# Five dot products moved ahead of the second half's turned rows, and the second unit's expert choice begun four items later

## The reference, cut to what matters

```
def peer_layer(h, w_q, keys, u, v):
    q = (h @ w_q).reshape(B, S, PEER_HEADS, 2, PEER_KEY_DIM)
    sc = jnp.einsum('bshpd,phnd->bshpn', q, keys)
    v1, i1 = lax.top_k(sc[..., 0, :], PEER_TOPK)          # 16 of 128
    v2, i2 = lax.top_k(sc[..., 1, :], PEER_TOPK)
    cand = v1[..., :, None] + v2[..., None, :]            # 256 sums
    cidx = i1[..., :, None] * PEER_N_KEYS + i2[..., None, :]
    best, pos = lax.top_k(cand, PEER_TOPK)
    gates = softmax(best)
    ...
        ue = jnp.take(u, it, axis=0)
        act = gelu(einsum('tkd,td->tk', ue, ht))
        ve = jnp.take(v, it, axis=0)
        return einsum('tk,tkd->td', gt * act, ve)
```

## Time and profile before

| what | us |
|---|---|
| three timed runs, median | 1663.82 |
| lowest and highest | 1662.99, 1665.97 |
| the profiled execution, span | 1766.8 |
| PE busy in it | 1526.0 (86%) |
| DVE busy | 1053.5 (60%) |
| ACT busy | 647.2 (37%) |
| POOL busy | 551.6 (31%) |
| mean granted clock of PE | 0.927 |

### The profile page before, as it was taken

How to read it: one execution, slowest core, us unless ns; L and a number is a source line. 1 busy time by engine, 2 the same in 40 slices (tenths; PEclk the granted TensorE clock), 3 DMA queues, 4 the chain that set the end, 5 groups by cost and what they waited for, 6 DMA issues and landing times.

```text
span 1766.8 us, 20473 instructions
## 1 busy us (share of the span) xinstructions
PE 1526.0 (86%) x8043; PEld 1152.1 (65%) x8043; DVE 1053.5 (60%) x1889; ACT 647.2 (37%) x1016; POOL 551.6 (31%) x607
## 2 busy tenths in 40 slices
PE   8999999998999999999999898796676775777684
PEld 7999897887797999988898765452222332333231
DVE  5655655786655655567456676375555564656563
ACT  5444535794453544446444232221111121111111
POOL 1000001210000100000100457666666657666663
PEclk9999999999999999999999688898788889888787
DMA  8555554343353555654345779989999989999995
GB/s 278 189 185 181 160 174 159 97 144 119 129 170 111 186 182 189 188 182 149 115 144 167 275 261 364 354 327 366 362 369 371 367 317 392 378 363 365 362 363 224
DMA packets 199945, 431.95 MB, mean 244 GB/s; under 512 B 20773, under 2 KB 114090, under 8 KB 199850
## 3 DMA queue, kind: packets, MB, share of 16 engines
q0 software_dynamic: 73728, 268.47, 39.4%
q1 hardware_dynamic: 123456, 159.92, 27.9%
q10 hardware_dynamic: 2666, 2.26, 0.4%
HBM read 429.55 MB, written 1.05 MB: 244 GB/s over the span
## 4 chain that ended last, share of the span: by engine, by line
PE 60%; DVE 17%; issue 10%; another core or an unknown queue 6%; ACT 6%; DMA 1%; POOL 0%; ACTq 0%; DVEq 0%
PE ps L403 60%; DVE GS L2449 3%; DVE WL L1712 3%; ACT WH L1210 2%; DVE RAW L2449 2%; DVE AR L2449 1%; DMA GS<-in_peer_u_dram,AR 1%; DVE AR L2300 1%; DVE AR L2296 1%; DVE H L1754 1%; DVE XN L1749 1%; DVE AR L2302 0%; DVE AR L2298 0%; DVE XL L1768 0%
## 5 line engine op out<-in xcount | busy, mean ns | idle before, releaser
L1712 DVE TENSOR_TENSOR WL<-RAW,WH 128x2048 fp32r<-128x2048 f32 x143 | 328.0, 2294 | 259.0 <-ACT WH L1210 257.0
L403 PE MATMUL ps<-XH,WH 128*128 128x256 f32 (+1 forms) x1448 | 424.9, 293 | 17.0 <-issue 7.3
L403 PE MATMUL ps<-XH,WL 128*128 128x256 f32 (+1 forms) x1448 | 417.5, 288 | 5.4 <-issue 5.4
L403 PE MATMUL ps<-XL,WH 128*128 128x256 f32 (+1 forms) x1448 | 417.4, 288 | 5.0 <-issue 5.0
L403 PE MATMUL ps<-GS,AR 128*128 128x512 f32 x576 | 298.2, 666 | 123.6 <-issue 88.3
L1210 ACT ACTIVATE WH<-RAW 128x2048 fp32r<-128x2048 f32 x137 | 262.4, 1915 | 183.0 <-PE ps L403 181.2
L403 PEld LDWEIGHTS ps<-GS,AR 128*128 128x128 f32 x576 | 120.1, 214 | 289.7 <-issue 247.2
L403 PEld LDWEIGHTS ps<-XH,WH 128*128 128x128 f32 x1448 | 285.5, 197 | 25.5 <-issue 16.9
L403 PEld LDWEIGHTS ps<-XH,WL 128*128 128x128 f32 x1448 | 285.9, 197 | 8.0 <-issue 8.0
L403 PEld LDWEIGHTS ps<-XL,WH 128*128 128x128 f32 x1448 | 285.8, 197 | 7.6 <-issue 6.8
L2501 POOL TENSOR_TENSOR small<-small 128x1 f32<-128x1 f32 x28 | 15.4, 557 | 708.2 <-DVE small L1744 365.7
(11 more groups left out here) (372 smaller groups left out, 1887.1 us busy)
## 6 DMA issues: line engine op xcount, KB each, us to landing
RAW<-in_ffn_w_gu_dram SPq DMA_DIRECT2D x44, 1024.0 KB, 5.2
RAW<-in_w_in_dram SPq DMA_DIRECT2D x39, 1024.0 KB, 5.2
RAW<-in_ffn_w_down_dram SPq DMA_DIRECT2D x22, 1024.0 KB, 4.8
RAW<-in_w_out_dram SPq DMA_DIRECT2D x12, 1024.0 KB, 4.8
RAW<-in_xa_wkv_dram SPq DMA_DIRECT2D x8, 1024.0 KB, 5.3
RAW<-in_w_peer_q_dram SPq DMA_DIRECT2D x8, 1024.0 KB, 5.4
RAW<-in_xa_wq_dram SPq DMA_DIRECT2D x4, 1024.0 KB, 7.1
RAW<-in_xa_wo_dram SPq DMA_DIRECT2D x4, 1024.0 KB, 5.0
```

The costliest lines, as they stand in the source:

```text
L403: return nc.tensor.matmul(out_, lhsT, rhs, start=start, stop=stop, skip_group_check=True)
L1712: nc.vector.tensor_tensor(conv(1, k, kt), v, conv(0, k, kt).bitcast(F32), ALU.subtract).then_inc(S["lo"], 1)
```

## The change

The dot products of items 0 to 4 are called in DVE's `query`, behind `choose_first` and ahead of `turn_half(1)`; the loop over items skips them. The generator of unit 1's choice is still made at item 0, but its steps begin at item 5: the condition for a step is now `j >= AHEAD and kk > 0`. On ACT the gates of unit 1 are made at item 9 and no longer at item 5; all later units keep rank 5. Nothing is added to or removed from what is computed.

```
+    AHEAD = 5
...
-            if kk == 5 and n + 1 < 16:
+            if kk == (5 if n else 9) and n + 1 < 16:
                 gates(n + 1)
...
-            if kk > 0:
+            if j >= AHEAD and kk > 0:
                 next(nxt[0], None)
...
+                for j in range(AHEAD):
+                    item(j)
                 turn_half(1)
...
             if what == "items":
                 for j in n:
-                    item(j)
+                    if j >= AHEAD:
+                        item(j)
```

## The result

| | median us | runs | lowest to highest |
|---|---|---|---|
| kernel before | 1664.46 | 4 | 1662.99 to 1665.97 |
| changed kernel | 1683.00 | 4 | 1682.54 to 1683.62 |

The ratio is 1.0105, with a 95% interval of 1.0088 to 1.0122: 18.5 us slower, where 8 were forecast. The time lies in the range, close to that of the rival in which PE's clock falls (1684.8).

A forecast was written before the change was run, and what follows sets the result against it. The prediction took the nearly unbroken stream of 512 gathers at 411 GB/s as the bound. PE later 4.0 plus indices 4.8, less some 0.8 covered, gave +8 us: 1671.8, range 1660.5 to 1686.

The forecast's parts named there:

- the rival in which PE's clock falls: PE's pause before the second-half query, about 987.3 to 992.4, halves its clock: 13 on top of 8, 1684.8; chance 0.22.
- The reading of the bound: From 977 us on, 512 gathers at 411 GB/s, nearly unbroken in timed runs; breaks at the stream's start count in full.
- The 103 us: Profiled 1766.8 us against timed median 1663.82; fifteen units at 5.1 us, 77 us, were taken as waits absent from timed runs.
- PE later by 4.0 us: Five dot products ahead of the second turn delay PE's second-half query from about 988.4 to 992.4; 0 to 4.0, taken 4.0.
- Early gathers, 0: POOL's gathers waiting for the early dot products' buffers go out sooner; gain 0 to 4.5 us, taken as 0.
- Indices, 4.8 us: Second unit's choice four items later delays row 16's gather, indices at 1037.7; price 3.2 to 4.8 us, taken 4.8.
- Gates, 0: Gates at item 9 cost ScalarE two table loads of 1.28 us; free, at most 2.6 us, or 5.3 by the skill page.
- The sum, +8: Whole kernel: 4.0 plus 4.8, less some 0.8 covered by queued transfers, gives +8 us, 1671.8; chance 0.36.
- first term: PE's second-half query starting 4.0 us later, on the premise that timed runs lack the profile's wait giving cover.

The follow-up runs named there:

- choice_late: Kernel before with only the second unit's choice begun at item 5 and its gates made at item 9, dot products unmoved; 1667.28 us, ratio 1.0023.
- filler8: Changed kernel plus eight idle products (matmuls nobody reads) on PE ahead of the second half's query; 1672.30 us, ratio 1.0044.
- filler8_dots_only: Changed kernel with the choice caught up by item 8, gates at item 6, and eight idle PE products ahead of the second-half query; 1670.48 us, ratio 1.0023.
- before_warm_2: Kernel before with one idle product in each of three short PE pauses, repeated at the usual condition; 1662.31 us, ratio 0.9986.

## Why the prediction was right or wrong

- **The reading of the bound** was right: the stream of gathers at 411 GB/s sets the end, and what breaks it between 1002 and 1040 is lost. The 103 us by which the earlier trace rows exceeds the timed runs were indeed not in them; unit periods of 45.94 us are 40.7 there.
- **PE later by 4.0 us**: mechanism right, size 5.5 (988.02 to 993.51). 0.4 of the difference is that PE started at 988.02 before, not at 988.4. The rest is that the first dot product waited 1.06 us for its gather and started at 986.69, not 986.04, and that the five took 6.08 us and not 5.7.
- **Early gathers, 0**: right. V2 to V4 went out without a wait, and the next wait grew to 8.75 us.
- **Indices, 4.8 us**: mechanism right, too large. 3.0 by choice_late, where U16 goes out 3.2 us later, the lower of the prediction's two figures; 1.8 between filler8 and filler8_dots_only, of which the second has a fall of the clock of its own. The 7.0 us from the weight piece to the index were right (1029.76 to 1036.79). That the index itself was placed well (1037.7 forecast, 1036.8 measured) was luck: the weight piece's end it was counted from, 1030.66, is 1014.15 in an undisturbed run, and the delays of PE and VectorE made up the rest.
- **Gates, 0**: right. PE goes from the first V rows to the next at 1033.10 without a wait, and behind the second load ScalarE waits 6.62 us for VectorE:

```profile
1028.93 1.28 ACT L1651 ACT_TABLE_LOAD   x1
1030.23 0.31 ACT L1651 ACTIVATE AR<-AR 128x16 f32<-128x16 f32 x1
...
1032.40 1.28 ACT L1681 ACT_TABLE_LOAD   x1
1040.30 0.21 ACT L1681 ACTIVATE AR<-AR 128x8 f32<-128x8 f32 x1 [6.62 <-DVE AR L2450]
```

- **The sum, +8**: with the clock held up (filler8) the change costs 7.6 us and runs at 1672.3, against a forecast of 1671.8. That they lie so close is in part luck: one term was too small and one too large, and the kernel before loses clock as well. Against before_warm_2, which does not lose it there, filler8 is 10.0 us slower (1672.3 and 1662.3).
- **The step that failed** is that the sum put the clock at nothing. Its first term took PE's 5.34 us pause to be absent from timed runs. On that premise the change makes a pause of about the same length, and the earlier trace rows showed half the clock behind such a pause. The prediction had this as a rival (0.22, against 0.36 for the forecast) and priced it at 13; its argument against it ("the clock may be low there in timed runs anyway") denies the premise of the first term. Whoever takes the 4.0 has to take the 13 as well. What the runs showed in place of nothing: the pause is 6.58 us, the clock is at half from 990.7 to 1021.4, and this costs 10.7 of the 18.5 us (filler8), where the rival had 13.

## What to carry to other kernels

An engine order that looks free because the engine idles there must be read for who else idles with it: the dot products fitted into VectorE's wait, but they pushed PE's input back, and the pause cost more in clock than in time. If a change lengthens a pause of PE, price the half clock behind it as a term of the sum, and try a few idle products in the pause before giving the reordering up. Where the profiled execution is far longer than the timed runs, list which of its waits the forecast takes as real, and use that list for every term alike.

## What was not expected of the hardware

- Pauses of PE of 3.3, 4.5 and 6.6 to 6.9 us at this place were followed by half the clock in the profiled run of each kernel that has them, and all 21 runs of these kernels have a mean clock of 0.991 or less. With six idle products (1.88 us of pause left in the profiled run) five of nine runs have 0.990 or less; with eight and no pause, none of seven (filler8). In before two pauses of 1.4 us differ: that ahead of 1002.74 left the clock at 1.00, that ahead of 1010.16, with one of 0.87 us soon behind it, was followed by half of it at 1011.1.
- Once down, the clock stayed at 0.50 for some 30 us, with PE nearly nine tenths busy or more in every stretch from 994 on. The end of it in the changed kernel:

```profile
1016.00:1020.00 4.00, 3.62 (x17) 3.62 (x18) 1.84 (x1) 3.78 (x4) 0.00 (x0) 0.50 0.14 57
1020.00:1021.40 1.40, 1.40 (x8) 1.40 (x8) 1.40 (x2) 0.00 (x0) 0.00 (x0) 0.50 0.00 0
1021.40:1024.00 2.60, 2.60 (x24) 2.60 (x23) 2.57 (x10) 0.21 (x1) 1.41 (x2) 1.00 0.91 255
```

The Trainium skill (TensorE: Matmul & The Clock Gate, Part 1) has activity release the throttle. The trace agrees that an idle PE loses its clock (here at 990.7, within the pause), but 27 us of work did not bring it back. Up to 1016 PE made products of 128 columns, and from 1017.3 on of 256. No run tests what brought the clock back at 1021.4, and that stays open.

- There is a condition, lasting through a whole group of runs, in which the kernel before takes 1767 instead of 1664 us, with pauses of 5 to 10 us on PE from 985 us on and none before but for the wait at the very start. The record gives one chip, 13, for that group and for the first, where the kernel before took 1664.24. Its cause stays open, and so does what the change would cost in it.
